# A four-layer transformer in one kernel: the differential layer's reciprocal roots move from GpSimd to ScalarE, two elementwise products from GpSimd to VectorE

## The reference, cut to what matters

```python
def project(h, rotary):                       # h_lat: 256 latent tokens, h_ctx: 256 context tokens
    q, k, v = jnp.split(h @ w_qkv, [...], axis=-1)
    q = rmsnorm_2(q.reshape(bsz, -1, 2, DIFF_HEADS, HEAD_DIM_2), q_norm)   # over 64 features of a head
    k = rmsnorm_2(k.reshape(bsz, -1, 2, DIFF_HEADS, HEAD_DIM_2), k_norm)
    if rotary:
        q, k = apply_rope(q, cos, sin), apply_rope(k, cos, sin)            # x*cos + rotated(x)*sin
    return q, k, v
...
p = softmax(q k^T / 8)                        # two maps of each head
a = p[:, 0] - lam * p[:, 1]
o = a v                                       # latents attend to latents and context
o = rmsnorm_2(o, subln) * (1.0 - lam_init)    # over the 128 features of a head
y = o @ w_o
```

## Time and profile before

| what | value |
|---|---|
| median of three runs | 1429.64 us (1428.9 to 1433.7) |
| the profiled execution: its own time, and the span of its records | 1429.12 us, 1427.8 us |
| TensorE busy | 1325.2 us (93%) |
| VectorE busy | 1051.8 us (74%) |
| ScalarE busy | 735.9 us (52%) |
| GpSimd busy | 103.9 us (7%) |
| chain that ended last, by engine | TensorE 65%, VectorE 17%, ScalarE 7%, DMA 5%, GpSimd 2% |
| granted TensorE clock, mean | 0.974 of full speed |

### The profile page before, as it was taken

One profiled execution on the slowest core, in us unless ns is written; L12 is line 12 of the kernel. 1 busy time (PEld: TensorE's weight loads), 2 busy tenths in 40 slices (PEclk: granted clock), 3 DMA queues, 4 the chain that ended last, 5 costly groups with the idle time before them and its releaser, 6 DMA issues.

```text
span 1427.8 us, 21925 instructions
## 1 busy us (share of the span) xinstructions
PE 1325.2 (93%) x8728; PEld 1186.7 (83%) x8728; DVE 1051.8 (74%) x1628; ACT 735.9 (52%) x1233; POOL 103.9 (7%) x146
## 2 busy tenths in 40 slices
PE   4899899999999799999767999789999899999998
PEld 3798799988797699997556776579998799899987
DVE  6777798887678588888656675778877697766643
ACT  3665755554856665543643654564444544644441
POOL 0022000000033000000023141200000000000000
PEclk9999999999999999999889999999999999999999
DMA  8865578679586346658612511438878566356551
GB/s 342 344 236 207 192 288 301 263 301 357 204 303 239 118 169 235 232 215 344 236 59 115 195 53 67 147 134 324 308 298 325 218 262 259 146 203 249 224 200 51
DMA packets 46310, 320.03 MB, mean 224 GB/s; under 512 B 5168, under 2 KB 5760, under 8 KB 8832
## 3 DMA queue, kind: packets, MB, share of 16 engines
q1 hardware_dynamic: 46208, 318.63, 59.0%
HBM read 317.51 MB, written 1.10 MB: 223 GB/s over the span
## 4 chain that ended last, share of the span: by engine, by line
PE 65%; DVE 17%; ACT 7%; DMA 5%; issue 4%; POOL 2%; SPq 0%; ACTq 0%; DVEq 0%; POOLq 0%
PE mat L596 13%; PE mat L598 13%; PE mat L597 13%; DVE wlo L1495 6%; PE mat L634 6%; PE mat L636 6%; PE mat L638 6%; DVE raw L1513 4%; ACT whi L1061 3%; DMA raw<-in_down 2%; PE mat L654 1%; POOL st L2083 1%; PE mat L953 1%; ACT tmp L1082 1%; PE mat L955 1%
## 5 line engine op out<-in xcount | busy, mean ns | idle before, releaser
L1495 DVE TENSOR_TENSOR wlo<-raw,whi 128x1024 fp32r<-128x1024 f32 x393 | 476.0, 1227 | 175.2 <-ACT whi L1061 173.9
L596 PE MATMUL mat<-hHL,whi 128*128 128x256 f32 x1864 | 533.2, 286 | 2.8 <-DVE tmp L1998 1.4
L597 PE MATMUL mat<-hHL,whi 128*128 128x256 f32 x1864 | 529.1, 284 | 0.0
L598 PE MATMUL mat<-hHL,wlo 128*128 128x256 f32 x1864 | 529.0, 284 | 0.0
L1061 ACT ACTIVATE whi<-raw 128x1024 fp32r<-128x1024 f32 x393 | 406.3, 1053 | 208.9 <-DMA raw<-in_down 70.0
L596 PEld LDWEIGHTS mat<-hHL,whi 128*128 128x128 f32 x1864 | 359.7, 193 | 8.9 <-issue 3.0
L597 PEld LDWEIGHTS mat<-hHL,whi 128*128 128x128 f32 x1864 | 359.7, 193 | 0.1
L598 PEld LDWEIGHTS mat<-hHL,wlo 128*128 128x128 f32 x1864 | 359.4, 193 | 0.0
L1513 DVE SCALAR_TENSOR_TENSOR raw<-raw,cB 128x1024 f32<-128x1024 f32 x192 | 234.1, 1228 | 8.0 <-DMA raw<-in_mod 8.0
L634 PE MATMUL mat<-whi,aHL 128*128 128x512 f32 x352 | 113.3, 392 | 1.9 <-DVE wlo L1495 1.9
L636 PE MATMUL mat<-wlo,aHL 128*128 128x512 f32 x352 | 112.3, 389 | 0.0
(11 more groups left out here) (207 smaller groups left out, 1511.0 us busy)
## 6 DMA issues: line engine op xcount, KB each, us to landing
raw<-in_mod SPq DMA_DIRECT2D x96, 1024.0 KB, 6.0
raw<-in_qkv SPq DMA_DIRECT2D x48, 1024.0 KB, 7.1
raw<-in_gate SPq DMA_DIRECT2D x44, 1024.0 KB, 5.1
raw<-in_up SPq DMA_DIRECT2D x44, 1024.0 KB, 5.6
raw<-in_down SPq DMA_DIRECT2D x44, 1024.0 KB, 5.6
raw<-in_wo SPq DMA_DIRECT2D x16, 1024.0 KB, 5.2
gtb<-gates SPq DMA_DIRECT2D x8, 512.0 KB, 7.0
cB<-in_crow SPq DMA_DIRECT2D x3, 512.0 KB, 8.0
```

Of the source, the lines that this page charges most:

```text
L596: pe.matmul(o, wh[:, k, :], hH[:, k, :], start=(k == 0), stop=False)
L597: pe.matmul(o, wh[:, k, :], hL[:, k, :], start=False, stop=False)
L598: m = pe.matmul(o, wl[:, k, :], hH[:, k, :], start=False, stop=(k == KT - 1))
L1495: dve.tensor_tensor(out=wlo[:, n % NSPL, :], in0=raw[:, f % NRAW, 1024 * h:1024 * h + 1024], in1=whi[:, n % NSPL, :].bitcast(f32), op=ALU. ...
```

## The change

The twelve norms of units, the two of the context and the sixteen of the outputs are made by ScalarE as exp(-0.5 * ln(mean + eps)), two instructions in a new helper `scalar_power`. The cosine product of a latent unit and the gain product of a context unit are made by VectorE. GpSimd has no instruction in this layer any more. In ScalarE's slot the new unit's copy and square now stand ahead of the copy of a turned unit (`scalar_unit` before `scalar_turn`).

```diff
@@ scalar_differential
                         act.activation(xn[:, t, :], cx[:, t, :], ACT.Square, accum_out=st[:, 250 + t:251 + t]
                                        ).then_inc(s_csq, 1)
+                    for t in range(2):
+                        scalar_power(st[:, 250 + t:251 + t], D, s_csq, t + 1, s_cpow, 2 * t + 1)
                 if u == 2:
                     gate_taken(2, 2)
+                if 0 < u <= len(UNIT_LIST):
+                    scalar_unit(u - 1)
                 if 0 <= u - 3 < len(UNIT_LIST) and UNIT_LIST[u - 3] in QKU:
                     scalar_turn(*UNIT_LIST[u - 3])
-                if 0 < u <= len(UNIT_LIST):
-                    scalar_unit(u - 1)
                 if u == 3:
                     for i in range(4):
                         scalar_ctx_group(i // 2, i % 2)
+                if 0 < u <= len(UNIT_LIST) and UNIT_LIST[u - 1] in QKU:
+                    i = QKU[UNIT_LIST[u - 1]]
+                    scalar_power(norm_stat(i), 64, s_dred, i + 1, s_drs, 2 * i + 1)
...
+        def scalar_power(ss, n, sem_in, value, sem_out, made):
+
+            act.wait_ge(sem_in, value)
+            act.activation(ss, ss, ACT.Ln, bias=epsc[:, :], scale=1.0 / n).then_inc(sem_out, 1)
+            act.wait_ge(sem_out, made)
+            act.activation(ss, ss, ACT.Exp, scale=-0.5).then_inc(sem_out, 1)
@@ scalar_diff_position
                 act.activation(weights_tile(n)[:, 0:P], diff_out(n), ACT.Square, accum_out=diff_stat(n, 7)).then_inc(s_xsq, 1)
+                scalar_power(diff_stat(n, 7), 128, s_xsq, n + 1, s_xpow, 2 * n + 1)
@@ vector_unit_norm
             if t >= 2:
+                dve.wait_ge(s_dn, i + 1)
+                if i >= 2:
+                    dve.wait_ge(s_qkt, i - 1)
+                dve.tensor_tensor(out=rope_tile(i).rearrange("p (h d) -> p h d", h=8), in0=yv,
+                                  in1=kgt[:, :].unsqueeze(1).to_broadcast([P, 8, 64]), op=ALU.mult).then_inc(s_ropp, 1)
                 return
@@ vector_unit_rope
             dve.wait_ge(s_ropv, ROPV[g, t] - 1)
+            dve.tensor_tensor(out=yv, in0=yv, in1=rope[:, 2 * (g % 3), t, :].unsqueeze(1).to_broadcast([P, 8, 64]), op=ALU.mult
+                              ).then_inc(s_ropp, 1)
             dve.wait_ge(s_ropp, ROPP[g, t])
             dve.tensor_tensor(out=rope_tile(i), in0=rope_tile(i), in1=unit_tile(i), op=ALU.add).then_inc(s_ropv, 1)
@@ pool_program: the powers of the context and of the outputs, and pool_unit with its power and its product, are gone
```

More of the change, by code:

```diff
@@ L1914, in vector_unit_rope @@
             i = QKU[g, t]
+            yv = unit_tile(i).rearrange("p (h d) -> p h d", h=8)
             dve.wait_ge(s_ropv, ROPV[g, t] - 1)
+            dve.tensor_tensor(out=yv, in0=yv, in1=rope[:, 2 * (g % 3), t, :].unsqueeze(1).to_broadcast([P, 8, 64]), op=ALU.mult
+                              ).then_inc(s_ropp, 1)
             dve.wait_ge(s_ropp, ROPP[g, t])
@@ L2034, in pool_program @@
                 pool_forgetting(h)
[L2035 to L2042, removed]
         def stick_diagonal(h):
@@ L2074, in pool_forgetting @@
                                channel_multiplier=1).then_inc(s_bm, 1)
[L2076 to L2094, removed]
         sync_program()
```

## The result

The changed kernel takes 1414.32 us (median of 4 runs, 1412.1 to 1417.1), the kernel before 1430.64 us beside it (4 runs): ratio 0.9882, 95% interval 0.9857 to 0.9906. The profiled execution took 1412.44 us, 16.7 less than the 1429.12 before; the sum had said 16.0 less.

The account below looks back on a forecast made before the run. Early, a serial chain on VectorE with GpSimd in its middle bounds the kernel; from 782 us TensorE does. Gains 11.7 + 6.0 less 1.7 make 16.0: 1429.1 - 16.0 = 1413.1, forecast 1413 us, range 1406 to 1421.

Parts of the forecast that it names:

- unit (1, 3), clock: TensorE's unit behind the first key's wait: with that gap gone it runs at full clock, gaining 1.5 us.
- early: Slots 1 to 7, a serial chain on VectorE through GpSimd: shortening it gains 11.7 us at unit (2, 2).
- slots 8 to 19: TensorE is the bound; two waits for weights, 4.3 us, go and 1.7 us of clock returns: 6.0 together.
- tail: Slots 20 to 29: the output's power delays a high part by 0.55 in slots 25, 26 and 28, losing 1.7 us.
- The power: VectorE's wait at a unit's norm: 0.65 us on ScalarE instead of 2.05 in early units, gaining 1.4 each.
- The product: Cosine product on VectorE: costs 0.72 us, replaces a 1.45 wait in four early latent units, gaining 0.73 each.
- My mark of wrong: Sign that the forecast fails: VectorE's added products start more than 0.7 us apart.
- Slots 1 to 3: TensorE 4.0 us ahead at the modulated context; the first key's 2.93 wait goes, making it 6.9 ahead.
- More: Rival, chance 0.12: other slow stretches of the early part shrink too, up to 5 us more, 1408 us.
- Less: Rival, chance 0.17: slot 3's key just too late, clock still drops, of later waits only 2.6 goes; 1419.5 us.
- Hidden: Rival, chance 0.06: TensorE, busy 93%, absorbs the gain; time within 4 us of before.
- Lockstep: Rival, chance 0.05: in-order ScalarE waits for VectorE's sums, delaying copies that free TensorE's banks; 13.5 us slots, 1447 us.

Follow-up runs that it names:

- powers_alone: Kernel before with all 30 powers on ScalarE, products still on GpSimd and ScalarE's old order: 1420.88 us, ratio 0.9918.
- slow_power: Changed kernel with three more logarithms, results unused, on ScalarE ahead of each unit's power: 1419.03 us, ratio 0.9906 to the kernel before.
- order_alone: Kernel before with only ScalarE's order changed, the new unit's copy and square ahead of the turned copy: 1430.24 us, ratio 0.9992.
- after_again: Changed kernel, unedited, timed and traced again: 1413.38 us, ratio 0.9882 to the kernel before.
- products_alone: Kernel before with only the cosine and gain products moved to VectorE, powers still on GpSimd: 1426.09 us, ratio 0.9953.
- tail_power_last: Changed kernel with the output's power behind the weight's high part on ScalarE in slots 25 to 28: 1413.46 us, ratio 0.9866 to the kernel before.
- all_but_order: Changed kernel with ScalarE's old order, turned copy before the new unit's copy: 1413.62 us, ratio 0.9870 to the kernel before.
- tail_and_mods: Changed kernel with slots 25 to 28's output power behind the high part, slots 2 and 3's modulation steps in VectorE's slot 3 wait: 1409.73 us, ratio 0.9837.
- gpsimd_outputs_and_mods: Changed kernel with the outputs' powers on GpSimd and the modulation steps of slots 2 and 3 moved into VectorE's context-split wait: 1410.89 us, ratio 0.9857.

## Why the prediction was right

From the common point, by traces of one execution each:

| Term | Predicted | Measured |
|---|---|---|
| to the modulated context, L972 (slots 1, 2) | 4.0 | 4.3 |
| to the key of slot 3, L987 | 2.9 | 3.3 |
| unit (1, 3), clock | 1.5 | 1.6 |
| to the first scores (low parts, context key) | 3.3 | 3.75 |
| **early** | 11.7 | 12.9 |
| slots 8 to 19 | 6.0 | 6.3 |
| tail | -1.7 | -2.2 |
| **all** | 16.0 | 17.0 |

The layer began 0.4 us later in the profiled execution, and that leaves 16.6, the difference of the spans.

**The power.** Taken at 0.65, measured 0.61 in each of the six early units and 0.35 in the last five, 0.50 as a mean; bounds 0.57 and 1.2. Where it lay on the path it was priced right, to 0.04. powers_alone shows that it carries most of the change, slow_power that it is on the path: 0.57 more per norm cost 2.0 us by the first scores, where all six in series would have cost 3.4.

**The product.** Taken at 0.72, measured 0.73 from start to start where the next operation reads the result (722.89 to 723.62), and 0.61 where it doesn't (723.62 to 724.23). My mark of wrong, "more than 0.7 us apart", was set tighter than my own term and says nothing. The rule of the Trainium skill (VectorE: DVE Perf Modes, The DRAIN you can't avoid), by which the prediction estimated some 0.4 us on top of 0.69, isn't borne out for 128x512 operations: neither pair is 1.1 apart.

**Slots 1 to 3.** Right in sum, and wrong twice in detail. TensorE now waits 0.52 for the copy of the first unit (719.29), which the four small instructions ahead of it on ScalarE delay; it costs nothing, since a wait of 3.19 follows. The prediction saw the delay and charged VectorE 0.2 for it, which didn't come either: the sums are level with before, and the low parts 2.16 ahead, not 1.9. And the wait of 2.93 did not go, it fell to 1.06. The prediction had VectorE reach unit (1, 0) in time by TensorE's old pace. But unit (1, 1) also came back to full rate earlier: before, it ran at half rate until 745.6, 6.0 us behind L972; now until 738.7, 3.0 behind. TensorE arrived at the turn 1.4 us earlier for that and waited for VectorE instead, so that clock gain was absorbed, as in order_alone. At L987 VectorE's schedule counts, 7.6 us ahead where the prediction had 7.2 for VectorE and 6.9 for TensorE; from L972 on that is 3.3. VectorE's schedule hangs in turn on when TensorE has done L972 and L987 in slot 2, and so on the clock there (after_again).

**The clock of unit (1, 3).** Right, and twelve traces agree. Behind a gap of 2.93, 2.99 or 3.52 us (before, powers_alone, products_alone) the unit took 7.57, 7.37 and 7.27; behind 2.08 (order_alone) 6.13, without the wait at its end; behind gaps of 0.46 to 1.57, and once behind none, 5.96 to 6.00 in the eight other traces. No run changed the gap alone, and elsewhere in these traces a shorter gap was enough (last section). The Trainium skill (TensorE: Matmul & The Clock Gate, HAM oscillation — how this bites in real kernels) has slow bursts follow idle gaps; this case's rows agree for the three gaps of 2.93 us and more.

**Slots 8 to 19.** Right: both waits for weights are gone, the clock is 1.00 from 810 to 868, and 6.3 us came back. The cover that I claimed for the exponentials is thinner than I said, though: in slow_power 0.57 us more per unit came out as waits of 0.58 and 0.97 us for ScalarE, so at these two places there was next to none.

**The tail.** The mechanism and the price per power are right (1.49 was predicted as 1.5, in slots 25 and 26). tail_power_last undoes it and recovers 0.56 at each of three places. Measured over the whole tail the loss is 2.2 in this pair of traces; between the five traces with the old tail (45.3 to 46.2 us long) and the five with the new (47.4 to 48.75) it is 2.1 in the means and 1.8 in the medians. The three waits account for 1.7; the kernel before has the shortest tail of its kind by 0.7, and the changed kernel's two traces differ by 1.2.

**The rivals.** *More* is refuted as to the time, though not in its first step. Gaps of 3.19 and 4.55 stayed, and with them the half-rate stretches behind, but these became shorter: the mean clock up to unit (2, 2), 717 to 771 us, is 0.94 where it was 0.87 (717 to 782), a loss of 0.06 x 54 = 3.2 us of clock instead of 8.5. Of what came back, the 1.4 of unit (1, 1) went into a wait for VectorE. *Less* fails at its condition: the clock of slot 3 came back though the key was late by 1.06. *Hidden* is refuted by the ratio. *Lockstep* is refuted in the changed kernel, with either order on ScalarE, and its beginning is seen in slow_power.

The early part's surplus of 1.2 us stands at known places: 0.3 at L972, the 0.2 that the first sums didn't cost among it; 0.4 more at L987; 0.1 of clock; and 0.45 behind it, where the low parts of slot 5 take 4.63 us instead of 5.72 without GpSimd beside them, which the prediction doesn't name. What stays open is how much of the 1.2 is scatter of the clock, which alone gave 0.8 at the first scores between two executions of one program (after_again), and how much of the low early part of products_alone. The errors of the three terms, 1.2 and 0.3 too little gain and 0.5 too little loss, are of the size of that scatter, so that the sum came within 1.0 us is partly luck; that each term came near is not.

## What to carry to other kernels

A wait of one engine for another's tiny instruction is priced by its whole round trip. Two ScalarE operations of 0.3 and 0.2 us took the place of a 1.65 us operation on GpSimd and gave 12 us: 8.4 because six such trips lay on a serial chain that TensorE stood behind, 6.0 because two later waits and the slow clock behind one of them went, less 2.1 in the tail. In this kernel a small power stood better behind the large operation that somebody waits for than ahead of it (three waits shorter by 0.56). And when a change shortens the path up to a wait, ask whether both sides of the wait move, since the later side decides.

## What was not expected of the hardware

The slow stretch behind a gap doesn't start and end at fixed distances from it. Behind L972 TensorE was back at full rate some 3.0 us after the restart in the changed kernel (gap 4.55), 3.7 in tail_power_last (4.29), 4.3 in all_but_order (4.28) and in after_again (4.29), 4.5 in slow_power (4.09) and 6.0 in the kernel before (5.83), and in three of them its first operation, L972, was still at full rate (0.63 us instead of 1.09). Nor does the length of the gap alone decide: behind 1.91 us at the same place TensorE ran at half rate until 3.9 us after the restart (tail_and_mods), behind 1.88 not at all (gpsimd_outputs_and_mods). A power that follows a square with its accumulator read costs the next instruction 0.56 us, though its two durations add to 0.49. A 128x1 operation of VectorE that meets a 128x512 product of GpSimd ends when the product ends (1.28 us instead of 0.22 where both start together, 0.53 where it starts 0.76 later), and two that fell inside a 128x1 power of GpSimd took 0.22.
